# Filter spectra from even and odd positions, and the late experts' order by the load of the fixed ones

## The reference

```python
def _bidir_long_conv(u, h_fwd, h_bwd):
    L = u.shape[1]
    n = 2 * L
    k = jnp.concatenate([h_fwd, jnp.zeros((1, D_MODEL), jnp.float32), h_bwd[1:][::-1]], axis=0)
    k_f = jnp.fft.rfft(k, n=n, axis=0)
    u_f = jnp.fft.rfft(u.astype(jnp.float32), n=n, axis=1)
    return jnp.fft.irfft(u_f * k_f[None], n=n, axis=1)[:, :L]

y = (_bidir_long_conv(u, h_fwd, h_bwd) + u * d_skip.astype(jnp.float32)) * x0.astype(jnp.float32)
...
    y = jnp.zeros_like(t)
    for e in range(N_EXPERTS):
        a, b = jnp.split(t @ w_up[e], 2, axis=-1)
        y = y + combine[:, e:e + 1] * ((jax.nn.silu(a) * b) @ w_down[e])
```

## Time and profile before

| | us |
|---|---|
| median of 3 runs | 1092.55 |
| lowest, highest | 1089.73, 1093.05 |
| the profiled execution | 1091.67 |
| its span in the profile | 1089.6 |
| PE busy | 1019.7 |
| DVE, POOL, ACT busy | 594.8, 318.6, 207.3 |

### The profile page before, as it was taken

How to read it: one execution, slowest core, us unless ns; L and a number is a source line. 1 busy time by engine, 2 the same in 40 slices (tenths; PEclk the granted TensorE clock), 3 DMA queues, 4 the chain that set the end, 5 groups by cost and what they waited for, 6 DMA issues and landing times.

```text
span 1089.6 us, 25741 instructions
## 1 busy us (share of the span) xinstructions
PE 1019.7 (94%) x10516; PEld 612.0 (56%) x10516; DVE 594.8 (55%) x1393; ACT 207.3 (19%) x497; POOL 318.6 (29%) x427
## 2 busy tenths in 40 slices
PE   8999999999899999999989999899979999999773
PEld 2545556565556666666555554575455666666442
DVE  6447897774743333333479991685574333333226
ACT  3142233002310000000240100562331000000002
POOL 1200000510145555555210000354014555555332
PEclk9999999999899999999989999699999999999997
DMA  9963467371999999999996886432096996999991
GB/s 331 402 240 116 176 251 289 127 273 75 350 397 406 406 405 406 357 406 406 369 367 255 327 302 235 149 103 69 10 364 257 407 406 263 383 402 405 406 356 58
DMA packets 101832, 319.00 MB, mean 293 GB/s; under 512 B 8417, under 2 KB 12705, under 8 KB 101377
## 3 DMA queue, kind: packets, MB, share of 16 engines
q1 hardware_dynamic: 91858, 299.65, 71.8%
q0 software_dynamic: 5776, 17.30, 4.7%
q10 hardware_dynamic: 4128, 1.05, 0.4%
HBM read 312.22 MB, written 5.77 MB: 292 GB/s over the span
## 4 chain that ended last, share of the span: by engine, by line
PE 78%; DVE 8%; DMA 6%; SPq 2%; POOL 2%; issue 2%; ACT 2%; DVEq 0%; ACTq 0%; POOLq 0%
PE bank L764 75%; DMA ring<-in_moe_w_down 4%; SPq L497 2%; POOL P L738 1%; PE bank L1203 1%; DVE st L1957 1%; DVE P L2017 1%; DVE hT L1735 1%; DMA group_row<-token_rows,rows_now 1%; DMA row_beta<-in_ln_b 1%; ACT x L1363 1%; PE bank L959 0%; DVE x L1761 0%; DVE x L2062 0%; PE bank L823 0%
## 5 line engine op out<-in xcount | busy, mean ns | idle before, releaser
L764 PE MATMUL bank<-ring,xgT 128*32 128x256 f32 x4224 | 243.0, 381 | 7.6 <-DMA ring<-in_moe_w_up 5.4
L764 PE MATMUL bank<-hT,ring 128*128 128x384 f32 x640 | 208.9, 489 | 2.1 <-DVE hT L1735 2.1
L764 PEld LDWEIGHTS bank<-ring,xgT 128*32 128x32 f32 x4224 | 146.2, 110 | 86.5 <-issue 8.6
L1922 DVE TENSOR_TENSOR he<-sa,bank 128x128 f32<-128x128 f32 x66 | 19.0, 288 | 297.6 <-ACT sa L1409 297.6
L764 PEld LDWEIGHTS bank<-hT,ring 128*128 128x128 f32 x640 | 122.2, 191 | 88.3 <-issue 5.3
L1559 DVE CUSTOM_DVE_ANT_0 ring<-ring,ring 128x1024 f32<-128x1024 f32 x120 | 146.8, 1224 | 4.6 <-PE bank L764 1.0
L764 PE MATMUL bank<-ring,heT 128*32 128x256 f32 x2112 | 129.0, 385 | 8.7 <-DMA ring<-in_moe_w_down 8.7
L764 PE MATMUL bank<-yg,ohT 32*128 32x256 f32 x1632 | 107.3, 391 | 3.4 <-DVE yg L1951 2.9
L764 PEld LDWEIGHTS bank<-ring,heT 128*32 128x32 f32 x2112 | 63.3, 110 | 64.4 <-issue 31.4
L718 POOL TENSOR_TENSOR yg<-ysb,gate_s 128x256 f32<-128x256 f32 x128 | 90.8, 731 | 19.5 <-ACT ysb L1414 12.0
L764 PEld LDWEIGHTS bank<-yg,ohT 32*128 32x128 f32 x1632 | 74.5, 184 | 36.4 <-issue 26.3
(11 more groups left out here) (279 smaller groups left out, 1108.0 us busy)
## 6 DMA issues: line engine op xcount, KB each, us to landing
ring<-in_moe_w_up SPq DMA_DIRECT2D x64, 2048.0 KB, 21.6
ring<-in_moe_w_down SPq DMA_DIRECT2D x32, 2048.0 KB, 18.5
ring<-in_k_ada SPq DMA_DIRECT2D x15, 2048.0 KB, 7.9
ring<-in_w_ada SPq DMA_DIRECT2D x9, 2048.0 KB, 14.6
ring<-in_na_w_qkv SPq DMA_DIRECT2D x6, 2048.0 KB, 11.7
ring<-in_hy_w_in SPq DMA_DIRECT2D x5, 2048.0 KB, 12.6
ring<-in_hy_w_out SPq DMA_DIRECT2D x2, 2048.0 KB, 13.6
ring<-in_na_w_out SPq DMA_DIRECT2D x2, 2048.0 KB, 9.6
```

The lines of the kernel that those rows point to most:

```text
L764: return nc.tensor.matmul(out, lhsT, rhs, start=first, stop=last)
L1922: v.tensor_tensor(he[:], sa[:], ps[0][:, 128:256], ALU.mult).then_inc(S["he_ready"], 1)
```

## The change

Two independent edits.

The sample's positions are reordered in the tables and in the filter's features: tile 1 holds the even positions, tile 2 the odd ones (`by_parity`), and the second tile of frequencies runs backwards (`mirrored`). The spectrum at the frequencies 0 to 127 is then the even part plus the odd part; at the mirrored ones it is even minus odd for the cosine and odd minus even for the sine. PE makes only the parts, 8 matmuls; ACT copies the odd parts to `K`, and DVE adds and subtracts (`sample_spectrum`). The prompt's spectrum is copied by ACT alone. `skip` is loaded as one row, and POOL adds it to position 0 of `hsum`, which adds it to the cosine at every frequency; PE waits for that with `skip_ready`. The transposes of u take every second column of the sample (`TOKENS_AT`).

For the experts, `turn_sign` is -2 where the first four experts hold more than 8.5 groups and 0 elsewhere, and the key becomes key x `turn_sign` + key. With -2 the signs are turned, and the late experts go smallest, largest, second smallest, second largest.

```diff
-TILE_AT = [1, PROMPT + 2, PROMPT + 2 + 128]
+TOKENS_AT = [slice(1, 1 + PROMPT), *(slice(PROMPT + 2 + k, PROMPT + 2 + k + 255, 2) for k in range(2))]
...
+FIRST_USUAL = 2 * FIRST
...
-    cs, ss = tables(SAMPLE)
+    by_parity = np.concatenate([np.arange(0, SAMPLE, 2), np.arange(1, SAMPLE, 2)])
+    mirrored = np.concatenate([np.arange(128), SAMPLE - 1 - np.arange(128)])
+    cs, ss = (m[:, mirrored] for m in tables(SAMPLE))
...
-                    sp.dma_start(skip[:], bass.AP(A["hy_d"].tensor, A["hy_d"].offset, [[0, 128], [1, D]])).then_inc(dft_in, 16)
+                    sp.dma_start(skip[0:1, :], bass.AP(A["hy_d"].tensor, A["hy_d"].offset, [[D, 1], [1, D]])).then_inc(skip_in, 16)
...
+            pool.wait_ge(skip_in, 16)
+            for t in range(2):
+                nc.gpsimd.tensor_tensor(hsum[0:1, t, :], hsum[0:1, t, :], skip[0:1, :], ALU.add).then_inc(skip_ready, 1)
...
-                    pe.wait_ge(dft_in, 32)
-                    for q in range(3):
-                        for h in range(2):
-                            out = [bank(G_AT[f"filtK{q}"] + 2 * h + r) for r in range(2)]
-                            spectrum_into(out, q, h, hsum, hdif)
+                    pe.wait_ge(dft_in, 16)
+                    pe.wait_ge(skip_ready, 2)
+                    for h in range(2):
+                        out = [bank(G_AT["filtK0"] + 2 * h + r) for r in range(2)]
+                        spectrum_into(out, 0, h, hsum, hdif)
+                    for h in range(2):
+                        cs = slice(h * 512, (h + 1) * 512)
+                        for r, src in enumerate((hsum, hdif)):
+                            for k in range(2):
+                                mm(bank(G_AT[f"filtK{1 + h}"] + 2 * r + k)[:, :], (Cs, Ss)[r][:, k, 0:128], src[:, 1 + k, cs]
+                                   ).then_inc(group_ready, 1)
...
-            to_tokens("ut", lambda j, t: uT[:, j, TILE_AT[t]:TILE_AT[t] + 128])
+            to_tokens("ut", lambda j, t: uT[:, j, TOKENS_AT[t]])
...
                 if n == 3:
-                    act.wait_ge(taps_ready, 3)
-                    for q in range(3):
-                        spectrum_sin(q)
+                    for h in range(2):
+                        for r in range(2):
+                            spectrum_copied(0, r, h, G_AT["filtK0"] + 2 * h + r)
+                    for h in range(2):
+                        for r in range(2):
+                            spectrum_copied(2, r, h, G_AT[f"filtK{1 + h}"] + 2 * r + 1)
...
+            def sample_spectrum(h):
+
+                hs = slice(h * 512, (h + 1) * 512)
+                for r in range(2):
+                    g = G_AT[f"filtK{1 + h}"] + 2 * r
+                    wait_evacuated(dve, g + 1)
+                    even, odd = ps[bank_of(g)][:, :], K[:, 2, r, hs]
+                    v.tensor_tensor(K[:, 1, r, hs], even, odd, ALU.add)
+                    a, b = ((even, odd), (odd, even))[r]
+                    v.tensor_tensor(odd, a, b, ALU.subtract).then_inc(evacuated[g % 8], 1)
...
                 if n == 3:
-                    for q in range(3):
-                        spectrum_cos(q)
-                    wait_group(dve, G_AT["filtK2"] + 3)
+                    sample_spectrum(0)
+                    sample_spectrum(1)
...
                 link(v.scalar_tensor_tensor(out=order_key[:], in0=blocks, scalar=float(EXPERTS), in1=iota, op0=ALU.mult, op1=ALU.subtract))
+                link(v.tensor_scalar(turn_sign[:], nbase[:, EXPERTS + FIRST:EXPERTS + FIRST + 1], FIRST_USUAL + 0.5, -2.0, ALU.is_gt, ALU.mult))
+                link(v.scalar_tensor_tensor(out=order_key[:], in0=order_key[:], scalar=turn_sign[:], in1=order_key[:],
+                                            op0=ALU.mult, op1=ALU.add))
```

More of the change, by code:

```diff
@@ L145, in tiles @@
         return m.reshape(m.shape[0] // 128, 128, m.shape[1]).transpose(1, 0, 2).reshape(128, -1)
-    cs, ss = tables(SAMPLE)
+    by_parity = np.concatenate([np.arange(0, SAMPLE, 2), np.arange(1, SAMPLE, 2)])
+    mirrored = np.concatenate([np.arange(128), SAMPLE - 1 - np.arange(128)])
+    cs, ss = (m[:, mirrored] for m in tables(SAMPLE))
     cp, sp = tables(PROMPT)
-    dft = np.concatenate([tiles(cs), tiles(ss), tiles(cs.T / SAMPLE), tiles(ss.T / SAMPLE),
+    dft = np.concatenate([tiles(cs[by_parity]), tiles(ss[by_parity]), tiles(cs.T / SAMPLE), tiles(ss.T / SAMPLE),
                           cp, sp, cp.T / PROMPT, sp.T / PROMPT], axis=1).astype(np.float32)
@@ L152, in shape_constants @@
     for L in (PROMPT, SAMPLE):
-        pos = np.arange(L, dtype=np.float32)[:, None]
+        pos = np.arange(L, dtype=np.float32)[by_parity if L == SAMPLE else slice(None), None]
         t = pos / np.float32(L - 1)
@@ L306, in build @@
         nbs = at("nbs", [128, NB_COLS], RM + 2176)
+        turn_sign = at("turn_sign", [128, 1], RM + 3776)
         order_key, order_rank, order_at, base_new = (at(n, [128, EXPERTS], RM + 3520 + 64 * i)
@@ L366, in build @@
         evacuated = [sem(f"evacuated{b}") for b in range(8)]
-        first_in, x_in, filt_in, rows_in, rows_moe_in, moe_in, att_in, dft_in = (
-            sem(n) for n in ("first_in", "x_in", "filt_in", "rows_in", "rows_moe_in", "moe_in", "att_in", "dft_in"))
+        first_in, x_in, filt_in, rows_in, rows_moe_in, moe_in, att_in, dft_in, skip_in, skip_ready = (
+            sem(n) for n in ("first_in", "x_in", "filt_in", "rows_in", "rows_moe_in", "moe_in", "att_in", "dft_in", "skip_in", "skip_ready"))
         scond_ready, mod_ready, scond_zero = sem("scond_ready"), sem("mod_ready"), sem("scond_zero")
@@ L1280, in condition_rows, with spectrum_copied @@
                 nc.scalar.activation(both, both, ACT.Silu).then_inc(sb_ready, 1)
[L1282 to L1286, removed]
+            def spectrum_copied(q, r, h, g):
+                wait_group(act, g)
+                nc.scalar.activation(K[:, q, r, h * 512:(h + 1) * 512], ps[bank_of(g)][:, :], ACT.Copy).then_inc(evacuated[g % 8], 1)
             def modulate_odd(name, l, shift, scale, dst=hT):
```

## The result

| | before | after |
|---|---|---|
| median of the runs | 1092.39 | 1077.36 |
| lowest, highest | 1089.73, 1093.05 | 1074.48, 1078.10 |
| the profiled execution | 1091.67 | 1074.48 |
| its span | 1089.6 | 1072.6 |

The change takes 15.0 us off the median; the ratio of the runs is 0.9859, with a 95% interval of 0.9837 to 0.9881. The forecast was 1078.0, in 1073.5 to 1084. The profiled execution of after is its fastest, so the two traces lie 17.0 us apart, 2 more than the medians.

The account below looks back on a forecast made before the run. TensorE was taken to bound the kernel (94% busy, 78% of the chain), then DMA in the tail. Terms -5.3 - 9.6 + 0.4 + 0.2 = -14.3 gave 1077.4 on the profiled execution, 1078 for a run; range 1073.5 to 1084.

Parts of the forecast that it names:

- The forecast's own case: Whole kernel: both the spectra and the order gain, giving 1075 to 1081 us; chance 0.62.
- rival of one half: Only the order works, 1082 to 1083 us, chance 0.12; or only the spectra work, 1086 to 1087 us, chance 0.11.
- The slower rival: At the spectra PE waits for POOL and a late skip row; 1095 us and more, chance 0.04.
- Spectra: Filter spectra before in_1: 8 matmuls replace 16, 6.9 us of PE removed, 5.3 gained; bounds 3.6 and 6.9.
- the idle: PE at the eighth product's bank, which ACT frees late: idles 2.1 us instead of 1.12.
- ACT's copies: Spectrum copies on ACT that free PE's banks: begin at 68.49 us and take 0.52 us each.
- the place of DVE's pair: DVE's add and subtract after ACT's fifth copy free in_1's bank, at 72.7 us with handovers.
- The stretch of half clock: At the spectra, added PE idle might bring half clock and take 1.7 us of the gain; only a bound.
- Order: Late experts of layer 1, turned: DMA gaps shrink, the stage ends 9.4 us earlier, taken as 9.6; bounds 6.5 and 11.2.
- the count of gaps: Layer 1's weight loads: last landing at 1049.4 instead of 1058.8 us; gaps of 10 + 2.4 us become 1 + 1.9.
- The two steps: Two more linked DVE steps in the ordering, 0.21 us each: cost 0.42 us in layer 1, 0.2 taken in layer 0.
- Strided transposes: Transposes of u reading the sample's columns with step 2: cost taken as 0, upper bound 2.3 us.

Follow-up runs that it names:

- the repeat: The changed kernel run once more unaltered, beside the kernel before on the same chip: 1076.89 us against 1091.88, ratio 0.9865.
- the spectra alone: The changed kernel without the turn of the late experts (turn_sign and its two steps left out): 1087.34 us, ratio 0.9960.
- the removed idle: The changed kernel with ACT's SiLU of the conditioning rows moved behind the spectrum copies of the fourth group: 1072.23 us, ratio 0.9815.
- the turn in both layers: The changed kernel with the bound of 8.5 groups set to 0.5, so layer 0 is turned too: 1084.40 us, ratio 0.9934.
- the two with half pieces: The changed kernel with half of each down piece loaded and used twice in layer 1: 1070.75 us with the turn, 1070.81 without it.

## Why the prediction was right, step by step
- **Which case.** The forecast's own case came, with both halves: 15.0 us against a sum of 14.3. That the two are so close is in part luck. The sum was made on the profiled execution, and there 17.2 us went (1091.67 to 1074.48). The spectra gave 1.2 us less than their term and the order 1.9 more (both below); 0.5 ahead of the first product, 1.0 in the attention stage and 0.7 in the first two groups of layer 1's experts (7.20 and 7.19 us in before, 6.85 and 6.82 in after) stood in no term. Neither rival of one half came: each part alone gave 4.5 and 8.8. The slower rival had no ground: skip's row landed by 41.1, since POOL began its adds there, and they were over at 45.8 where PE asks at 59.4. They took 2.34 us each, less than the 3.6 of the prediction.

```profile
L642 POOL TENSOR_TENSOR hsum<-hsum,skip x2: 2340/2340/2341, 41.1 to 43.4; 1x1024 f32<-1x1024 f32 x2
```

- **Spectra: 5.3 forecast, 4.1 measured.** The 6.9 us of removed products, the idle (2.1 forecast, 1.89 measured), ACT's copies (0.52 forecast, 3.01/6 = 0.50) and the place of DVE's pair were right. The stretch of half clock, held as a bound at 1.7 us, did occur, and did in the repeat and in the spectra alone; it should have been in the sum, which would then have been 3.6. With the removed idle it is gone, and in_1 follows at 10.42 us. For the same reason PE did not end within 0.2 us of the ACT and DVE chain: DVE's first pair ended at 71.9, PE at 73.8. Without half clock they would have stood nearly level, as worked out.
- **Order: 9.6 forecast.** The last down piece was used 9.8 us earlier against the start of place 4 (172.9 us after it in the earlier trace rows, 163.1 now), where the count of gaps gave 9.4. The times of issue behind the gaps were met: counted from place 4's start, place 8's down piece was worked out at 38.0 us and issued at 38.1, place 10's at 72.4 and issued at 72.4; place 15's was to land at 163.5 and was used at 163.1. PE's waits were 3.8 us, and with 1.6 us of half clock it lost 5.4 where I had 5.6. The end of the last expert gained 11.5 us from place 4's start, not 9.6. The prediction's own numbers say so: 17 us lost before less 5.6 is 11.4. I had taken the shift of the last landing, 9.4, and with it kept the stretch of half clock that before has behind that landing (10.3 us from there to the end, 8.6 in after); its absence I had only in the upper bound. As a part of the whole the order gave 8.8 us by the medians, although it gave 11.1 in its stage. In its trace 1.2 us were lost ahead of that stage, between layer 0's last combine and layer 1's first expert; the two steps account for some 0.5 of them, the rest lies within the scatter of the attention stage (below).
- **The two steps: 0.42 forecast, 0.46 measured**, in the timeline of DVE in layer 1 (order_key to pairs 0.67 us, where the earlier trace rows has 0.21):

```profile
807.94 0.18 DVE L1887 SCALAR_TENSOR_TENSOR order_key<-nbase,mc 128x16 f32<-128x16 f32 x1
808.15 0.15 DVE L1888 TENSOR_SCALAR turn_sign<-nbase 128x1 f32<-128x1 f32 x1
808.34 0.23 DVE L1889 SCALAR_TENSOR_TENSOR order_key<-order_key,turn_sign 128x16 f32<-128x16 f32 x1
808.61 0.31 DVE L1891 TENSOR_TENSOR pairs<-order_key 128x144 f32<-128x144 f32 x1
```

  In layer 0 the lead over before stood at 4.4 us ahead of the ordering, 4.0 at the first expert and 4.3 behind the last: they cost 0.4 at first, 0.2 of it came back over the experts, and 0.1 to 0.2 is left, as taken.
- **Strided transposes: 0 forecast, 0.15 measured.** The stage took 2.99 us instead of 2.84. The weight loads did get longer, 0.141 to 0.205 us in the median:

```profile
L830 PEld LDWEIGHTS bank<-first,uT x24: 139/205/209, 182.7 to 185.3; 128*128 128x128 f32 x24
```

  For 16 strided loads that makes 1.0 us, of which 0.15 shows; the rest is hidden beside the matmuls. The Trainium skill, "SBUF — State Buffer", section "Door 1: The DMA port swizzle", has a step of up to 4 fp32 as free; the row speaks against free for the load itself, and the sum was safe only through the overlap.
- **What the sum had not.** One us was gained in the attention stage up to the row of layer 1's norm; the diff does not touch that stage. Before has the longer stretch of half clock there: over the same work, 684 to 708 us in before and 680 to 704 in after, 0.64 of the clock is granted against 0.72, some 1.8 us of full clock. First before, then after:

```profile
684.00:708.00 24.00, 20.93 (x122) 12.63 (x121) 14.56 (x61) 11.99 (x53) 8.51 (x10) 0.64 0.43 133
```
```profile
680.00:704.00 24.00, 20.53 (x134) 12.90 (x136) 15.72 (x65) 12.73 (x56) 8.66 (x11) 0.72 0.44 138
```

  But farther on it is the other way round (796 to 812 us: 0.89 of the clock in before, 0.79 in after), and over the whole of the attention layer, 540 to 820 us, the two lose 15.4 and 15.3 us of full clock. From layer 0's last combine to layer 1's first expert product the ten kernels of the study take 285.0 to 287.1 us, before 285.8 and after 285.2; the two longest, which have one part of the change each, lost 15.4 us to the clock as well. So this is scatter of 1 to 2 us, and the clock alone does not explain it; its cause stays open. The 0.5 us ahead of the first product is scatter too: the repeat of the changed kernel has that product at 60.15 us, after at 59.37.

## What to carry to other kernels
A ring of weights over experts of unequal load is a matter of gaps: write down when each load's slot comes free, count the stretches in which the loader has nothing to do, and set the end by the last gap plus the pieces behind it; that gave the last landing here to 0.4 us. Which order is good depends on what stands ahead of the first large expert: behind nine groups small first gained 11 us, behind four it lost 9. So it needs a condition and not a habit. When matmuls are removed, look for what they had covered on the other engines: here a SiLU that had cost 1.35 us cost 4.0 afterwards, and moving it behind the urgent copies gave those back in the stage. And look at what the lead meets next: in the trace half of that lead was waited away at the weights of layer 0.

## What the runs showed of the hardware that was not expected
- An idle of 1.12 us on PE between 60 and 70 us brought no half clock before; one of some 1.9 us did, in all six kernels that had it (after and its repeat, the spectra alone, the turn in both layers, the two with half pieces), and none of the other four had half clock there. The 1.9 us of waiting cost another 1.7 us by the clock. That the idle is the cause is shown by one pair only, the changed kernel with and without the SiLU moved.
- Transposes whose source columns stand two floats apart load their 128 x 128 floats in 0.205 us instead of 0.141 and lengthen the stage by only 0.15 us.
- POOL's add over 1024 elements of a single partition takes 2.34 us.
